# High and low parts of the second projections' weight units by converting and accumulating transfers

## What is computed

```
ff = square(relu(hn @ w_up)) @ w_down                     # first block, 1024 -> 4096 -> 1024
a, u = split(h @ w_ffn_in)                                # second block, 1024 -> 2 x 2816
a = causal_dwconv(a, conv_w, conv_b)
x = x + (silu(a) * u) @ w_ffn_out                         # 2816 -> 1024
```

## Time and profile before

| | |
|---|---|
| median of two runs | 1435.78 us |
| profiled execution | 1436.38 us, span 1434.3 us |
| TensorE (PE) busy | 1419.2 us, 99% |
| VectorE (DVE) busy | 965.0 us, 67% |
| ScalarE (ACT) busy | 639.3 us, 45% |
| GpSimd (POOL) busy | 215.3 us, 15% |
| mean DMA traffic | 91 GB/s, q1 share 28.5% of 16 engines |
| mean granted clock | 0.997 |

### The profile page before, as it was taken

The page is one execution under the profiler, slowest core; times in us unless marked ns, Lnnn a source line. Parts: engine busy times, 40 slices in busy tenths (PEclk is TensorE's granted clock), DMA queues, the critical chain, the costliest instruction groups (busy, mean ns, idle before and its releaser), DMA issues.

```text
span 1434.3 us, 20178 instructions
## 1 busy us (share of the span) xinstructions
PE 1419.2 (99%) x7910; PEld 1210.9 (84%) x7910; DVE 965.0 (67%) x1501; ACT 639.3 (45%) x1000; POOL 215.3 (15%) x136
## 2 busy tenths in 40 slices
PE   9999999999999999999999999999999999999998
PEld 6776898889989888887899788888888888999887
DVE  5777477877677657887686726434463767777884
ACT  5345544544435424545464546323342544444440
POOL 4175324000000012330152105000021000000000
PEclk9999999999999999999999999999999999999999
DMA  6222113333323432222121212332322333332332
GB/s 240 89 74 74 59 60 90 103 102 103 104 89 104 133 96 71 84 88 74 59 60 45 65 43 71 103 103 89 103 89 92 97 96 101 99 103 89 99 108 74
DMA packets 36350, 129.98 MB, mean 91 GB/s; under 512 B 4040, under 2 KB 4296, under 8 KB 36256
## 3 DMA queue, kind: packets, MB, share of 16 engines
q1 hardware_dynamic: 35968, 128.44, 28.5%
q10 hardware_dynamic: 288, 0.26, 0.1%
HBM read 126.56 MB, written 2.10 MB: 90 GB/s over the span
## 4 chain that ended last, share of the span: by engine, by line
PE 89%; DVE 6%; ACT 2%; issue 1%; DMA 1%; SPq 0%; DVEq 0%; ACTq 0%
PE P L1729 18%; PE P L1730 17%; PE P L1731 17%; PE P L1710 4%; PE P L1712 4%; PE P L1711 4%; PE P L1777 4%; PE P L1768 4%; PE P L1770 4%; PE P L2070 1%; DVE WL L2563 1%; PE P L1817 1%; PE P L1818 1%; PE P L1819 1%; PE P L1748 1%
## 5 line engine op out<-in xcount | busy, mean ns | idle before, releaser
L2157 ACT ACTIVATE WH<-WR 128x1024 fp32r<-128x1024 f32 x215 | 227.2, 1057 | 282.3 <-PE P L1731 205.7
L2563 DVE TENSOR_TENSOR WL<-WR,WH 128x1024 fp32r<-128x1024 f32 x199 | 268.1, 1348 | 117.0 <-ACT WH L2157 116.6
L1729 PE MATMUL P<-AH,WH 128*128 128x512 f32 x520 | 211.7, 407 | 0.1
L1731 PE MATMUL P<-AH,WL 128*128 128x512 f32 x520 | 203.6, 392 | 0.0
L1730 PE MATMUL P<-AL,WH 128*128 128x512 f32 x520 | 203.4, 391 | 0.0
L1729 PE MATMUL P<-FH,WH 128*128 128x512 f32 x432 | 168.4, 390 | 0.2 <-ACT WH L2157 0.2
L1730 PE MATMUL P<-FL,WH 128*128 128x512 f32 x432 | 168.3, 390 | 0.0
L1731 PE MATMUL P<-FH,WL 128*128 128x512 f32 x432 | 168.0, 389 | 0.0
L3378 POOL TENSOR_TENSOR AC<-AC,SQ 128x512 f32<-128x512 f32 x27 | 42.4, 1571 | 507.7 <-ACT SQ L2212 506.8
L1729 PEld LDWEIGHTS P<-AH,WH 128*128 128x128 f32 x520 | 98.1, 189 | 23.8 <-issue 4.5
L1731 PEld LDWEIGHTS P<-AH,WL 128*128 128x128 f32 x520 | 98.0, 188 | 21.4
(11 more groups left out here) (409 smaller groups left out, 3028.5 us busy)
## 6 DMA issues: line engine op xcount, KB each, us to landing
WR<-in_ws SPq DMA_DIRECT2D x215, 512.0 KB, 3.6
WX<-in_ws SPq DMA_DIRECT2D x18, 512.0 KB, 3.6
out<-Y SPq DMA_DIRECT2D x8, 256.0 KB, 2.0
H<-in_xT SPq DMA_DIRECT2D x3, 512.0 KB, 7.8
C<-in_const SPq DMA_DIRECT2D x1, 946.5 KB, 10.9
H<-in_xT SPq DMA_DIRECT2D x2, 256.0 KB, 4.1
PR<-in_pT SPq DMA_DIRECT2D x1, 512.0 KB, 4.7
WR<-in_ws SPq DMA_DIRECT2D x1, 384.0 KB, 4.3
```

Of the source, the lines that this page charges most:

```text
L1729: e.matmul(P, wh, xh, start=start, stop=False)
L1731: ins = e.matmul(P, wl, xh, start=False, stop=stop)
L2157: e.activation(H, w_source(m, order, k), ACT.Copy).then_inc(*at.up("w_hi", "w_hi", k))
L2563: e.tensor_tensor(L, w_source(m, order, k), H, ALU.subtract).then_inc(*at.up("w_lo", "w_lo", k))
```

## The change

The plain units that lie between the first and the last pair of each MLP, 30 in all, get their parts without raw buffer, without `w_hi` and without `w_lo`:

- GpSimd issues a transfer from the chunk in DRAM to `WH`, which converts float32 to float32r (`w_hi_dma`). It waits for `("w_used", k - 4)`.
- ScalarE writes the negated high part to `WL` (`w_minus`). It waits for the landing of that transfer.
- GpSimd issues a second transfer from the same chunk to `WL` that adds to what is there (`w_lo_dma`). It waits for `w_minus`. TensorE waits for its landing where it waited for VectorE's `w_lo`.

The steps stand at the places in the list where `w_hi` and `w_lo` of those units stood. The 30 raw loads fall away. Some semaphores are shared by more steps of the same engine, which makes room for eight new ones.

```
+        self.by_dma = set()
+        for s in "25":
+            mine = [c for c, at in sections if at == s]
+            if mine and s in "25":
+                self.by_dma.update(k for c, k in self.unit_of.items() if mine[0] < c < mine[-1])
...
+            if self.unit_of.get(c) in self.by_dma:
+                self.raw.append(None)
+                self.raw_before.append(None)
+                continue
...
-            self.say("w_hi", k)
+            self.say("w_hi_dma" if k in self.by_dma else "w_hi", k)
+            if k in self.by_dma:
+                self.say("w_minus", k)
...
-            self.say("w_lo_pool" if self.onpool else "w_lo", k)
+            self.say("w_lo_dma" if k in self.by_dma else "w_lo_pool" if self.onpool else "w_lo", k)
...
+    def w_minus(k):
+        w.wait_ge(*at("w_hi", k))
+        e.activation(m.WL[:, k % NW, :], m.WH[:, k % NW, :].bitcast(F32), ACT.Copy, scale=-1.0).then_inc(
+            *at.up("w_minus", "w_minus", k))
...
+    def w_hi_dma(k):
+        w.wait_ge(*at("w_used", k - NW))
+        e.dma_start(m.WH[:, k % NW, :], m.dram["ws"][order.units[k][1]]).then_inc(
+            *at.up(f"w_hi_dma{k % NW}", "w_hi", k, by=16))
+
+    def w_lo_dma(k):
+        w.wait_ge(*at("w_minus", k))
+        e.dma_start(m.WL[:, k % NW, :], m.dram["ws"][order.units[k][1]], accum_op=ALU.add).then_inc(
+            *at.up(f"w_lo_dma{k % NW}", "w_lo", k, by=16))
```

More of the change, by code:

```diff
@@ L287, in rest @@
             kind, c = self.units[k]
-            self.say("w_lo_pool" if self.onpool else "w_lo", k)
+            self.say("w_lo_dma" if k in self.by_dma else "w_lo_pool" if self.onpool else "w_lo", k)
             if kind == 0:
                 self.say("s_add", c, 4)
-            elif kind != 2:
+            elif kind != 2 and k not in self.by_dma:
                 self.load(c + 1 if kind == 1 else c)
@@ L298, in load @@
             self.say("w_load", c)
-            if c + 1 < NCHUNK and self.raw_before[c + 1] is None:
+            if c + 1 < NCHUNK and self.raw_before[c + 1] is None and self.raw[c + 1] is not None:
                 self.say("w_load", c + 1)
@@ L2049, in values2 @@
                                stop=q == nk - 1)
-        ins.then_inc(*at.up("values2", "values2", u))
+        ins.then_inc(*at.up("values", "values2", u))
         if n == 3:
@@ L2249, in scale1 @@
         w.wait_ge(*at("recip1", u))
-        e.activation(p, p, ACT.Copy, scale=m.ST1[:, 6 + 3 * u:7 + 3 * u]).then_inc(*at.up("probs1", "probs1", u))
+        e.activation(p, p, ACT.Copy, scale=m.ST1[:, 6 + 3 * u:7 + 3 * u]).then_inc(*at.up("probs", "probs1", u))
     def turned1(u, t):
@@ L2257, in turned1 @@
             w.wait_ge(*at("values1", u - 2))
-        e.activation(m.PT1[:, u % 2, 0:W], m.bank[t.bank][:, 0:W], ACT.Copy).then_inc(*at.up("turned1", "turned1", u))
+        e.activation(m.PT1[:, u % 2, 0:W], m.bank[t.bank][:, 0:W], ACT.Copy).then_inc(*at.up("turned", "turned1", u))
         at.also(("turned1", u), "read", t.id)
@@ L2398, in scale2 @@
             e.activation(s, s, ACT.Copy, scale=m.WST[:, 10 * u + 8 + g:10 * u + 9 + g]).then_inc(
-                *at.up("probs2", "probs2", u))
+                *at.up("probs", "probs2", u))
     def turn2(u, t):
@@ L2406, in turn2 @@
             w.wait_ge(*at("values2", u - 2))
-        e.activation(m.PT2[:, u % 2, 0:W], m.bank[t.bank][:, 0:W], ACT.Copy).then_inc(*at.up("turned2", "turned2", u))
+        e.activation(m.PT2[:, u % 2, 0:W], m.bank[t.bank][:, 0:W], ACT.Copy).then_inc(*at.up("turned", "turned2", u))
         at.also(("turned2", u), "read", t.id)
@@ L2529, in ffn_u @@
             ffn_split(f)
-    run = {"s_snap": s_snap, "up_second": up_second, "t_u": t_u, "t_split": t_split, "up_split": up_split,
+    run = {"w_minus": w_minus, "s_snap": s_snap, "up_second": up_second, "t_u": t_u, "t_split": t_split, "up_split": up_split,
            "ffn_tap": ffn_tap, "ffn_silu": ffn_silu, "ffn_second": ffn_second, "ffn_split": ffn_split,
@@ L2723, in qk1 @@
             if q < 2:
-                e.scalar_tensor_tensor(o, ps, 0.125, rb, ALU.mult, ALU.mult).then_inc(*at.up("qk1", "qk1", q))
+                e.scalar_tensor_tensor(o, ps, 0.125, rb, ALU.mult, ALU.mult).then_inc(*at.up("qk", "qk1", q))
             else:
-                e.tensor_tensor(o, ps, rb, ALU.mult).then_inc(*at.up("qk1", "qk1", q))
+                e.tensor_tensor(o, ps, rb, ALU.mult).then_inc(*at.up("qk", "qk1", q))
         at.also(("qk1", q), "read", t.id)
@@ L2982, in gk_low @@
         e.tensor_tensor(m.PT2[0:16, 0, :], m.bank[t.bank][0:16, :], m.RBC3[0:16, :], ALU.mult).then_inc(
-            *at.up("gk_low", "gk_low"))
+            *at.up("gk", "gk_low"))
         at.also(("gk_low",), "read", t.id)
@@ L2988, in gk_split @@
         e.tensor_tensor(m.GX[32:48, :], m.PT2[0:16, 0, :], m.GX[0:16, :].bitcast(F32), ALU.subtract).then_inc(
-            *at.up("gk_split", "gk_split"))
+            *at.up("gk", "gk_split"))
     def gk_rest():
@@ L2995, in gk_rest @@
         e.tensor_tensor(m.GKR[r, :], m.GKU[r, :], m.GKR[r, :].bitcast(F32), ALU.subtract).then_inc(
-            *at.up("gk_weights", "gk_weights"))
+            *at.up("gk", "gk_weights"))
     def va_in(t):
@@ L3004, in gk_up @@
         e.tensor_scalar(m.BC[:, hh, :], m.bank[t.bank][:], m.p("b_gk", hh), None, ALU.add).then_inc(
-            *at.up("gk_up", "gk_up", hh))
+            *at.up("gk", "gk_up", hh))
         at.also(("gk_up", hh), "read", t.id)
@@ L3558, in clear4 @@
             did("clear4", s)
-    run = {"t_diff": t_diff, "w_lo_pool": w_lo_pool, "square": square, "ple_gated": ple_gated, "ple_sum": ple_sum, "clear1": clear1, "glu_gate": glu_gate,
+    run = {"t_diff": t_diff, "w_lo_pool": w_lo_pool, "w_hi_dma": w_hi_dma, "w_lo_dma": w_lo_dma, "square": square, "ple_gated": ple_gated, "ple_sum": ple_sum, "clear1": clear1, "glu_gate": glu_gate,
            "pool_sums": pool_sums, "pool_means": pool_means, "rsq": rsq, "sc_taps": sc_taps, "sc_b": sc_b, "ple_in": ple_in, "gk_weights": gk_weights, "lv_clear": lv_clear,
```

16 lines of the change are left out of this document (8 added, 8 removed).

## The result

The changed kernel took 1627.47 us, the median of two runs (1623.96 to 1630.98), against 1435.78 us: ratio 1.1335, 95% interval 1.1299 to 1.137. Forecast were 1620 us, range 1530 to 1765. The profiled execution has a span of 1629.2 us, 194.9 us more than before.

A forecast was written before the change was run, and what follows sets the result against it. The prediction took TensorE, busy 99% of the span, as the bound. It added 122 us for double cycles, 38 for single ones and 24 for the clock, 184 us, to 1436.4 us: 1620 us, range 1530 to 1765.

The forecast's parts named there:

- What bounds the kernel: Whole kernel: TensorE, busy 99% of the span; removing VectorE's 40 us of subtractions worth 0, at most 4.7 us.
- Double cycles: Twelve pairs with two plain units behind them: product 4 starts 10.2 us late each, 122 us in all.
- The adding transfer: GpSimd's second transfer, to the low buffer: 6.2 us from issue to landing, ends 3.3 and 9.4.
- Single cycles: Six pairs with one plain unit: low part lands 6.3 us late, holding a 3 us late product 4; 38 us.
- The clock: Work after each long TensorE stall runs at half clock: 2 us, 12 times, 24 us; 0 for the six shorter ones.
- Quick transfers: Rival: GpSimd's transfers are about as fast as SP's, 1509 to 1550 us; chance 0.17.
- Slow transfers: Rival: converting and adding run well under a plain copy's rate, or half clock lasts longer; 1700 us and up; chance 0.18.
- The lock by VectorE: One way to slow transfers: VectorE keeps GpSimd from making descriptors, 1.35 us at each issue; 65 us more, 1685 us.
- Not slower: Rival: the waits fit in the 4.1 us of slack before slot 6, leaving VectorE's relief, 1432 us; chance 0.03.

The follow-up runs named there:

- experiment 12: The kernel before with, in the second MLP, the split of a pair's result said two ticks later, behind the next pair's first copy: 1431.72 us, ratio 0.9978.
- experiment 9: The changed kernel with a second transfer that only converts and does not add: 1584.05 us, ratio 1.1032.
- the filler: The changed kernel with idle matmuls before product 4, ten where two plain units follow a pair, two where one does: 1606.49 us, ratio 1.1205.

## Why the prediction was right, and where it was off

- **What bounds the kernel.** Right: VectorE's 40 us (measured 27 less busy time: the subtractions sum to 36 us less, other instructions to more) were worth nothing. At most 4.7 us were to be won, and experiment 12 wins about 3.
- **Double cycles.** Forecast 12 x 10.2 = 122 us, measured 121.3. The path is as forecast, but the sum is better than its terms, which is luck in part. The first high transfer lands after 3.7 to 5.7 us, 4.3 on average, where 4.6 was forecast. GpSimd sends the next transfer 0.55 us after the adding one, where I had 1.0; the second high transfer then lands after 6.1 to 6.8 us, 6.3 on average, forecast 6.2. Against these gains stands a term that I had put at nothing: the adding transfer goes out some 0.4 us after the negation's end (326.13 to 326.51 in the cycle shown).
- **The adding transfer.** Forecast 6.2 us, measured 5.4; of which adding is 1.6 (experiment 9), as forecast from the data part's 1.67 us. What was too high is the 1 us for making descriptors: a transfer that only converts lands after 3.8 us (experiment 9), against 3.6 for SP's.
- **Single cycles.** Forecast 6 x 6.3 = 38 us, measured 32.6, in a wait of 2.2 to 3.7 us for the copy and one of 1.8 to 4.5 us for the low part. The prediction has both.
- **The clock.** This is the mis-sized term: 24 us forecast, some 41 read from the trace (45 with the rest that has no row). For a double cycle 2 us were forecast; 2.5 is the part of its length that is not waiting, 27 / 12 = 2.3 the clock's own reading, 2.1 what filling takes away: nearly right. For the single cycles I took 0, and it is 12 us for six, 2 each. The clock falls there too: the window 1463.4 to 1465.5, right after such a wait of 2.7 us, was granted 0.50, as the last line of the block behind this list shows. The trace of before had the warning, a fall some 3 us after the last matmul, about the length of each idle time in a single cycle.

Windows of one single cycle of the changed kernel, columns as above:

```profile
1462.00:1463.40 1.40, 0.00 (x0) 0.00 (x0) 0.21 (x1) 1.40 (x4) 0.76 (x1) 0.88 0.00 0
1463.40:1465.50 2.10, 2.02 (x9) 2.02 (x10) 2.10 (x4) 0.98 (x2) 0.12 (x1) 0.50 0.67 92
```

By the Trainium skill, TensorE: Matmul & The Clock Gate, Part 1, the clock comes back after sustained activity; the trace agrees, with 0.50 while TensorE was at work from 335.2 to 338 and 1.00 from 341.

- **Rivals.** *Quick transfers:* the converting one is nearly as quick as SP's, 3.8 against 3.5 us, but the adding one is not. The Trainium skill, DMA: Bandwidth & Descriptors, Anatomy of one DMA, gives one fit for transfers issued by GpSimd and does not tell the two kinds apart; it makes 3.2 us here (an estimate). The measured 3.8 and 5.4 us lie above it and apart, and the measurement decides. *Slow transfers:* the high transfer behind an adding one takes up to 6.8 us, yet that was in the sum. The lock by VectorE (the Trainium skill, SBUF — State Buffer, the "DVE blocks DMA" trap) is not seen: the adding transfer's issue takes 0.87 to 0.90 us all 30 times, 18 of them beside a VectorE instruction. VectorE stands still through 26 of the 30 issues of high transfers, and those 18 and the other 4 are all of one kind (TENSOR_TENSOR), so this run is a weak test of the lock. *Not slower* needed 0.8 us per transfer; the shortest landing of one was 3.7 us.
- **The total.** 122 + 38 + 24 = 184 against 121 + 33 + 45, less the 4.5 us that were there before, 195. The errors of the last two terms, 5 too much and some 20 too little, partly cancel, so that the total is nearer (1620 against 1627 us) than the terms deserve.

## What to carry to other kernels

Work that is moved from an engine to a transfer must be priced by what it does after its buffer comes free, not by the engine time it saves. With a prefetched raw copy and two conversions that was 2.7 us (0.3 to the start, 1.05 and 1.35), with two transfers in series it is 12 us (319.8 to 332.1 in the cycle shown), and the lead was 5.6. Look next at what stands behind each new wait in its engine's queue: two orders of the same transfers differed by some 56 us. Before such a change, ask whether the relieved engine bounded anything at all; here TensorE's waits for it in the two stretches summed to nothing. And count the clock with each wait: even the short ones, of 2 to 4 us, brought a loss of about 2 us in each single cycle.

## What was not expected of the hardware

- An adding transfer of 512 KB to SBUF takes 5.4 us to landing and a converting one 3.8, with SP's plain one at 3.5. The adding one slows what runs beside it: a high transfer issued 0.5 us behind it took 6.1 to 6.8 us, and 4.5 to 4.8 behind one that does not add.
- The same adding transfer took 8.1 us (median) beside three raw loads and 5.5 us when these waited. 55 us of kernel time hung on it.
- Idle times of only 2.7 us in single cycles were followed by work at a granted clock of 0.50. The size, 12 us over six cycles, is read from the trace; the filler took 4 of them away, and no run all.
